# The final norm's stores issued by ScalarE instead of SyncE, in a one-core encoder layer

## What is computed

```python
def rmsnorm(x, g):
    x32 = x.astype(jnp.float32)
    y = x32 * lax.rsqrt(jnp.mean(x32 * x32, axis=-1, keepdims=True) + RMS_EPS)
    return (y * g.astype(jnp.float32)).astype(x.dtype)

def encoder_trunk(x, ...):
    for l in range(DEPTH):          # DEPTH is 1
        x = x + jnp.concatenate([y_pool, y_lru, y_conv], axis=-1) @ w_out[l]
        x = x + expert_choice_ffn(rmsnorm(x, norm2_g[l]), router_w[l], exp_w_gate[l], exp_w_up[l], exp_w_down[l])
    return rmsnorm(x, final_g)
```

## Time and profile before

| | us |
|---|---|
| median of 3 runs | 2803.96 (2800.8 to 2804.36) |
| the profiled execution | 2789.21 |
| its span, first to last instruction | 2787.3 |
| busy: TensorE matmul | 2513.2 (90%) |
| busy: VectorE | 1714.3 (62%) |
| busy: ScalarE | 1133.1 (41%) |
| busy: GpSimd | 502.6 (18%) |
| final norm, from the issue of its first load to the span's end | 2725.84 to 2787.3 |

### The profile page before, as it was taken

The page is one execution under the profiler, slowest core; times in us unless marked ns, Lnnn a source line. Parts: engine busy times, 40 slices in busy tenths (PEclk is TensorE's granted clock), DMA queues, the critical chain, the costliest instruction groups (busy, mean ns, idle before and its releaser), DMA issues.

```text
span 2787.3 us, 43273 instructions
## 1 busy us (share of the span) xinstructions
PE 2513.2 (90%) x15947; PEld 2209.0 (79%) x15947; DVE 1714.3 (62%) x2209; ACT 1133.1 (41%) x1532; POOL 502.6 (18%) x349
## 2 busy tenths in 40 slices
PE   6999899963999449999999999999999999999980
PEld 4454455542888339999999999999999999999980
DVE  4499756675333657557557557557557557657534
ACT  4101455551222114444444444444444444444423
POOL 0000022230000011312311312312312312312210
PEclk9999999986999669999999999999999999999995
DMA  5000011124544127767768668668668668668638
GB/s 173 16 18 13 36 50 34 34 77 118 164 150 151 38 78 198 186 163 218 183 164 220 181 165 218 181 166 218 181 167 219 179 167 221 177 168 223 170 77 279
DMA packets 641858, 406.74 MB, mean 146 GB/s; under 512 B 27840, under 2 KB 620992, under 8 KB 640704
## 3 DMA queue, kind: packets, MB, share of 16 engines
q1 hardware_dynamic: 614080, 366.96, 45.6%
q0 software_dynamic: 27648, 37.77, 7.1%
HBM read 348.04 MB, written 56.62 MB: 145 GB/s over the span
## 4 chain that ended last, share of the span: by engine, by line
PE 80%; DVE 11%; issue 3%; ACT 2%; DMA 2%; SPq 1%; POOL 0%; DVEq 0%; ACTq 0%; POOLq 0%
PE ps L1124 40%; PE ps L1141 20%; PE ps L944 8%; PE ps L1014 6%; DVE rows L1233 6%; PE ps L898 1%; DMA y<-fin_y 1%; PE ps L1031 1%; PE ps L919 1%; PE ps L932 1%; ACT rows L766 1%; SPq L515 1%; DVE fin_y L1609 0%; PE ps L1072 0%; SPq L504 0%
## 5 line engine op out<-in xcount | busy, mean ns | idle before, releaser
L1124 PE MATMUL ps<-x_h,w_l 128*128 128x288 f32 x2816 | 830.4, 295 | 20.0 <-issue 20.0
L1124 PE MATMUL ps<-x_l,w_h 128*128 128x288 f32 x2816 | 828.8, 294 | 0.0
L1124 PE MATMUL ps<-x_h,w_h 128*128 128x288 f32 x2816 | 828.8, 294 | 0.0
L1477 DVE TENSOR_TENSOR w_l<-raw,w_h 128x1024 fp32r<-128x1024 f32 (+1 forms) x480 | 637.3, 1328 | 277.2 <-ACT w_h L834 276.6
L834 ACT ACTIVATE w_h<-raw 128x1024 fp32r<-128x1024 f32 (+1 forms) x480 | 545.3, 1143 | 453.1 <-PE ps L1141 272.3
L1124 PEld LDWEIGHTS ps<-x_h,w_l 128*128 128x128 f32 x2816 | 529.3, 188 | 20.0 <-issue 20.0
L1124 PEld LDWEIGHTS ps<-x_l,w_h 128*128 128x128 f32 x2816 | 529.3, 188 | 0.0
L1124 PEld LDWEIGHTS ps<-x_h,w_h 128*128 128x128 f32 x2816 | 529.2, 188 | 0.0
L624 POOL DMA_INDIRECT resid<-y_rows,idx_cur x144 | 250.2, 1738 | 964.9 <-ACT y_rows L849 930.4
L1141 PE MATMUL ps<-h_h,w_h 128*128 128x288 f32 x1408 | 414.0, 294 | 0.0
L1141 PE MATMUL ps<-h_h,w_l 128*128 128x288 f32 x1408 | 414.0, 294 | 0.0
(11 more groups left out here) (212 smaller groups left out, 2491.0 us busy)
## 6 DMA issues: line engine op xcount, KB each, us to landing
raw<-w_gate SPq DMA_DIRECT2D x176, 512.0 KB, 4.2
raw<-w_up SPq DMA_DIRECT2D x176, 512.0 KB, 4.6
raw<-w_down SPq DMA_DIRECT2D x128, 704.0 KB, 5.8
n_x<-x SPq DMA_DIRECT2D x18, 512.0 KB, 3.9
mix_in<-mixed SPq DMA_DIRECT2D x18, 512.0 KB, 4.8
s_x<-x SPq DMA_DIRECT2D x18, 512.0 KB, 5.4
resid<-s_r SPq DMA_DIRECT2D x18, 512.0 KB, 3.3
tokens<-s_h SPq DMA_DIRECT2D x18, 512.0 KB, 5.2
```

Source lines behind the costliest of these rows:

```text
L1124: ins = e.matmul(ps[:, bank, 0:SLOTS], lhs(k), rhs[:, k, 0:SLOTS], start=m == 1, stop=m == 3 * KD)
L1477: e.tensor_tensor(w_l[:, m % SPLIT, 0:k * P], raw[:, m % RAW, 0:k * P], w_h[:, m % SPLIT, 0:k * P].bitcast(F32), ALU.subtract).then_inc(lo ...
```

## The change

Stores of the final norm are issued by ScalarE. The store of tile t stands in ScalarE's program behind the squares and the root of tile t + 1; the last store stands alone at the end. SP's block keeps the 18 loads, one behind the other, each with its wait for `f_y`. Waits, semaphores, buffers and the transfers themselves stay as they are.

```diff
@@ SP
-            def f_store(t, p):
-                e.wait_ge(f_y, t + 1)
-                apart(e, passed)
-                e.dma_start(y[bass.ds(t * P, P), :], fin_y[:, p, :]).then_inc(f_st[p], 16)
-            for t in range(2):
+            for t in range(4):
                 f_load(t, t)
-            f_load(2, 2)
-            f_load(3, 3)
             with e.Fori(0, NT // 4 - 1) as i:
                 for q in range(4):
-                    f_store(4 * i + q, q % 2)
                     f_load(4 * i + q + 4, q)
-            for t in range(NT - 6, NT - 4):
-                f_store(t, t % 2)
-                f_load(t + 4, t % 4)
-            for t in range(NT - 4, NT):
-                f_store(t, t % 2)
+            for t in range(NT - 2, NT):
+                f_load(t, t % 4)
@@ ScalarE
+            def f_store(t, p):
+                e.wait_ge(f_y, t + 1)
+                apart(e, passed)
+                e.dma_start(y[bass.ds(t * P, P), :], fin_y[:, p, :]).then_inc(f_st[p], 16)
+
             def f_tile(t, q, k):
                 e.wait_ge(fx_ld[q], 16 * k + 16)
                 rms(fin_x[:, q, :], fin_sq[:], 2, q, f_sd)
+                if not (isinstance(t, int) and t == 0):
+                    f_store(t - 1, (q - 1) % 2)
             ring_tiles(e, f_tile, step, 4)
+            f_store(NT - 1, 1)
```

## The result

| | before | after |
|---|---|---|
| median us | 2802.29 (2800.8 to 2804.36, 7 runs) | 2811.0 (2808.81 to 2813.23, 7 runs) |
| ratio | | 1.0031, 95% interval 1.0019 to 1.0042 |
| final norm: issue of the first load to the end of the span, in the profiled execution | 2725.84 to 2787.3: 61.5 | 2742.44 to 2811.4: 69.0 |

The kernel is slower by 8.7 us, more than the 5.6 us that the prediction took as the least that can be told from no change. The profiled execution of before was a quick one (2789.2 us against a median of 2802.3), and what makes it so lies ahead of the final norm: the stage begins 16.6 us earlier there than in the profile after. So the spans of the two profiles must not be compared; the stages can be, and they differ by 7.5 us.

A forecast was written before the change was run, and what follows sets the result against it. The prediction took store landings, every second one a rung of the final norm's chain, as the bound. Its terms, 0 for SP, 0 for ScalarE and 4.0 us for slower landings, added to 2803.96 gave 2808.0 us, range 2799 to 2813.

The forecast's parts named there:

- What bounds: Final norm: every second store's landing delays VectorE's next write; eight such landings (rungs of a ladder) total 33.4 us.
- SP without the stores: SP's queue in the final norm: 14 loads begin 0.62 us earlier, nothing gains by it; gain 0.
- ScalarE with the stores: ScalarE's program in the final norm: store issues of 0.62 us stay hidden; price 0, upper bound about 0.2 us.
- The store's way through the DMA engines: Stores sharing DMA engines with loads from another queue: 0.5 us more per landing, eight rungs, 4.0 us lost.
- The sum: Whole kernel: 0 + 0 + 4.0 us on the 2803.96 median gives 2808.0 us.
- the slower rival: Final norm's DMA queues: loads regularly ahead of stores, 8 us lost, 2812.0 us; chance 0.24.
- The loads get in front: Final norm's DMA queues: load packets regularly first, landings 5.0 us, 8 us lost, 2812.0; chance 0.24.
- Nothing moves: DMA engines in the final norm: their rate binds or waiting stores go next, time stays 2804.0 us; chance 0.25.
- Two queues move more than one: DMA engines in the final norm: one queue's packets fill the other's gaps, 6.8 us gained, 2797.1; chance 0.13.

The follow-up runs named there:

- e5: Kernel before with four fin_y output buffers in place of two, still one queue, store then load: 2793.65 us against 2802.36 (0.997).
- e6: The change with four fin_y output buffers in place of two, so two queues: 2795.47 us against 2802.36 for the kernel before (0.9975).
- e2: The change, but load t+4 waits until ScalarE has issued store t, so the store goes first: 2801.65 us against 2798.45 before (1.0013).
- e1: The change, but ScalarE also issues the loads after the first four, each behind a store, on one queue: 2799.46 us against 2798.45 before (1.0004).
- e9: The change with only half of each load from the fifth tile on, layer not computed: 2805.59 us against 2802.07 before (1.0011).
- e10: The change without the 14 loads from the fifth tile on, layer not computed: 2791.3 us against 2802.07 before (0.9961).
- e8: The change itself, measured a second time: 2810.97 us against 2802.36 for the kernel before (1.0028).
- e4: The change, but load t+4 waits on SP until store t has landed: 2808.56 us against 2798.45 for the kernel before (1.0039).
- e3: Kernel before with SP's order turned round, load t+4 then store t, one queue: 2807.82 us against 2798.45 (1.0035).
- e7: The change, but load t+4 waits for the root of tile t+2, some 2 us behind the store: 2803.66 us against 2802.36 before (1.0004).

## Why the prediction was right, and where it was off

- *What bounds.* Right: the ladder of landings sets the stage. e5 and e6 show it from the other side, since a longer landing is free once it is no rung.
- *SP without the stores: gain 0.* Right about the gain. But here the 0.62 us by which the loads moved forward was priced only for the loads, and in the term of the store's way only as sharing. e2 gives it back on two queues and is 6.5 us of stage shorter than the change: the load's position is the larger part of the price.
- *ScalarE with the stores: 0.* Right (e1). From its issue to the next squares it takes 0.42 us in one turn and 0.72 in the next, about SP's 0.62; VectorE's waits for the root in the stage are 0.5 us. (The root of tile 2, put at 2735.9, sums to 2736.0 from the times given; nothing hangs on it.) That a slip of tile 1's store doesn't matter, since the odd tiles "aren't the ladder", was wrong: they became it, and the store that landed after 6.78 us is tile 1's.
- *The store's way through the DMA engines.* The mechanism, even sharing by two queues, is seen in the packets (51 to 50), and e9 and e10 show that the load beside it is what lengthens the store's way. The term was mis-sized: 0.5 us a landing had been taken and 1.1 came in the median (4.0 to 5.1); by the chain it is 39.8 less 33.4 us, 0.8 a rung, although the last rung is free of loads. The step that failed is the estimate of 4.3 to 4.5 us for a shared landing. It put 2 x 524 KB at 345 GB/s behind a start of usual length; but on the rungs of tiles 3 to 11 a store issued at once with a load starts 0.7 to 1.0 us later than a lone one, behind the load's slow first packets, on tile 13 over 2 us later, and the steady rate fell to 299 GB/s.
- *The sum.* 4.0 us forecast, 7.5 and 6.7 us in the stage, 8.7 and 8.6 us in the medians. The loss is more than twice the forecast's. The time of 2811.0 lies within the range and only 3.0 us above the 2808.0, since the median of before came out 1.7 us under the 2803.96 that the sum began with. That the range holds it is owed to its having been drawn around the slower rival, not to the forecast's term. That it can be told from no change (0.31%) had been given 0.27.
- *The rivals.* "The loads get in front" gave the better number, 2812.0, from landings of 5.0 us, and was right for the start of the rungs (13 to 29 of the load's packets ahead of the store's first, on tiles 3 to 11 of the profile after and of e8, and 113 on tile 13); for the rest of its way the store is level with the load. The 5.0 it took from the loads' median is no shown cause of the 5.1. "Nothing moves", and with it the rule of the Trainium skill (DMA: Bandwidth & Descriptors, "Issuing engines are not separate DMA queues"), holds for the rate: e5 and e6 have equal stages. For the time of this kernel, where a landing is waited for, it doesn't give "nothing moves": the same rule's "interleave" is part of what lengthens the landing. "Two queues move more than one" found nothing: 299 GB/s, not more than 345, and 383 in both e5 and e6. The trace doesn't agree for this loop with the advice of the Trainium skill (Perfetto Trace Analysis, "DMA Optimizations").

What stays open: the two comparisons give 8.7 and 8.6 us, the stages 7.5 and 6.7. The other 1 to 2 us lie outside the final norm or in the spread of single executions. All seven profiles with loads on SP's queue and stores on ScalarE's (after, e2, e4, e6 to e9) are 1.2 to 2.3 us worse against before by their medians than by their stages, those with one queue (e1, e3, e5) -0.4 to 0.6 us. No run was made that takes this apart. Nor is it shown why the load's first packets are slow, or why they go ahead although a lone store's first packet comes after 0.8 us and the load's here after 1.0. No run exchanges the two queues, so it isn't shown whether it is the load or SP's queue that goes first.

## What to carry to other kernels

A single queue is also an order: the transfer that is waited for goes ahead of the one that isn't. Whoever moves one of them to another engine's queue gives this order up, and where the same semaphore lets both go, the one that is waited for can start behind the other and then shares the engines with it: here it landed after 5.1 us in place of 4.0, while the load landed 4.9 us behind its issue in place of 5.0. Look whether a landing is a rung of the chain; if so, add a buffer first (here 8.7 us for 8 KB per partition), after which the choice of queue hardly matters; if there is no room, keep them on one queue in the order of need, or let the urgent one go 0.6 us ahead, which here took back all but 3.2 us. And sum the landings that are rungs: in e4 and e7 the median of all stores fell below before's, while the rungs grew in e4 and shrank by only 0.6 us in all in e7.

## What the runs showed of the hardware

- A store of 512 KB to HBM with nothing beside it landed 2.6 or 2.7 us after its issue, 18 times out of 18 (e10).
- With a 512 KB load issued on another queue at the same moment it landed in 5.1 or 5.0 us (after, e8), with a load of 256 KB in 4.4 (e9), with a load 0.6 us behind in 4.3 (e2); medians of 18 stores, the last of which have no load beside them.
- When both began on idle engines, the load's first packets took 0.5 us each (23 packets, 71.5% of a microsecond of 16 engines), and the store had 2 packets in that time (after, 2776 to 2777 us).
- With the load issued 0.16 us ahead, 113 of its 128 data packets started before the store's first one (tile 13, after and e8).
- Two queues with work moved 383 GB/s, and so did one (e6, e5), though the median store landed 1.5 us later with two.
